# A fifth quad by seven products in the gate/up pairs, its low parts made by GpSimd, the residual parked in DRAM

## The reference

```python
for l in range(DEPTH):                                  # DEPTH = 2
    h = rmsnorm(x, norm_mix[l])
    q, k, v, gate_b, gate_c, u = split(h @ w_in[l])     # 2048 x 6144
    o_attn = diff_attention(rope(q), rope(k), v, lam)   # 8 heads, then a sub-norm
    o_conv = short_gated_conv(gate_b, gate_c, u, conv_w[l])
    x = x + concat(o_attn, o_conv) @ w_out[l]           # 2048 x 2048
    h = rmsnorm(x, norm_ffn[l])
    x = x + (silu(h @ w_gate[l]) * (h @ w_up[l])) @ w_down[l]   # 2048 x 5632, twice; 5632 x 2048
return rmsnorm(x, norm_final)
```

## Time and profile before

| | |
|---|---|
| runs | 2156.14, 2156.8, 2157.34 us |
| profiled execution, span from first to last instruction | 2155.3 us |
| TensorE, VectorE, ScalarE, GpSimd busy | 2144.2, 1771.7, 1218.7, 314.5 us |
| weights and all else read from memory | 448.65 MB, 209 GB/s |
| granted TensorE clock, mean | 0.999 |

### The profile page before, as it was taken

The page is one execution under the profiler, slowest core; times in us unless marked ns, Lnnn a source line. Parts: engine busy times, 40 slices in busy tenths (PEclk is TensorE's granted clock), DMA queues, the critical chain, the costliest instruction groups (busy, mean ns, idle before and its releaser), DMA issues.

```text
span 2155.3 us, 27924 instructions
## 1 busy us (share of the span) xinstructions
PE 2144.2 (99%) x10397; PEld 1794.4 (83%) x10397; DVE 1771.7 (82%) x2143; ACT 1218.7 (57%) x1714; POOL 314.5 (15%) x310
## 2 busy tenths in 40 slices
PE   9999999999999999999999999999999999999998
PEld 7888888888888888888888888888888888888886
DVE  5776676899899988999866666768998998988997
ACT  6454455666566555556554555546665665655564
POOL 0031120211221110000001211201112112100010
PEclk9999999999999999999999999999999999999999
DMA  9654445777777776767766444557777777756685
GB/s 349 203 183 176 176 157 189 212 218 223 246 217 229 227 229 205 227 216 221 246 200 217 171 161 157 176 194 212 218 229 232 219 222 244 221 198 219 219 240 181
DMA packets 152872, 456.81 MB, mean 212 GB/s; under 512 B 17440, under 2 KB 18080, under 8 KB 152352
## 3 DMA queue, kind: packets, MB, share of 16 engines
q1 hardware_dynamic: 132624, 416.41, 55.5%
q0 software_dynamic: 18816, 35.66, 9.8%
q10 hardware_dynamic: 1296, 2.94, 0.4%
HBM read 448.65 MB, written 2.10 MB: 209 GB/s over the span
## 4 chain that ended last, share of the span: by engine, by line
PE 97%; DVE 1%; ACT 1%; DMA 1%; POOL 0%; issue 0%; ACTq 0%; SPq 0%; DVEq 0%
PE bank L1861 16%; PE bank L1863 16%; PE bank L1862 16%; PE bank L1835 14%; PE bank L1875 9%; PE bank L1874 9%; PE bank L1873 9%; PE bank L1838 7%; PE bank L2039 1%; PE bank L1998 1%; PE bank L2021 1%; PE bank L1977 0%; DMA raw<-w_gu_dram 0%; POOL o_rms L675 0%; DVE wlo L1191 0%; PE bank L2007 0%
## 5 line engine op out<-in xcount | busy, mean ns | idle before, releaser
L761 ACT ACTIVATE whi<-raw 128x1024 fp32r<-128x1024 f32 x540 | 553.9, 1056 | 195.2 <-PE bank L1863 137.4
L1184 DVE TENSOR_TENSOR wlo<-raw,whi 128x1024 fp32r<-128x1024 f32 x504 | 606.9, 1229 | 65.9 <-ACT whi L761 64.9
L767 ACT ACTIVATE whi<-raw 128x1024 fp32r<-128x1024 f32 x480 | 430.0, 944 | 241.7 <-DVE raw L1206 139.6
L1191 DVE TENSOR_TENSOR wlo<-raw,whi 128x1024 fp32r<-128x1024 f32 x480 | 501.0, 1084 | 49.7 <-ACT whi L767 46.4
L1835 PE MATMUL bank<-xg,whi 128*128 128x512 f32 x1280 | 406.9, 399 | 1.0 <-DVE wlo L1440 1.0
L1861 PE MATMUL bank<-whi,xg 128*128 128x512 f32 x864 | 339.3, 393 | 0.5 <-DVE wlo L1184 0.5
L1863 PE MATMUL bank<-whi,xg 128*128 128x512 f32 x864 | 336.7, 390 | 0.0
L1862 PE MATMUL bank<-wlo,xg 128*128 128x512 f32 x864 | 336.5, 389 | 0.0
L1838 PEld LDWEIGHTS bank<-xg,wlo 128*128 128x128 f32 x1280 | 240.5, 188 | 56.9
L1838 PE MATMUL bank<-xg,wlo 128*128 128x256 f32 x1280 | 252.0, 278 | 0.0
L1835 PEld LDWEIGHTS bank<-xg,whi 128*128 128x128 f32 x1280 | 195.0, 189 | 3.3 <-DVE xg L1434 1.4
(11 more groups left out here) (161 smaller groups left out, 3050.7 us busy)
## 6 DMA issues: line engine op xcount, KB each, us to landing
raw<-w_gu_dram SPq DMA_DIRECT2D x268, 512.0 KB, 4.9
raw<-w_in_dram SPq DMA_DIRECT2D x188, 512.0 KB, 4.5
raw<-w_down_dram SPq DMA_DIRECT2D x140, 512.0 KB, 5.4
raw<-w_gu_dram SPq DMA_DIRECT2D x168, 256.0 KB, 4.2
raw<-w_out_dram SPq DMA_DIRECT2D x64, 512.0 KB, 4.4
raw<-w_gu_dram POOLq DMA_DIRECT2D x84, 256.0 KB, 5.7
raw<-w_down_dram SPq DMA_DIRECT2D x72, 256.0 KB, 4.7
raw<-w_down_dram POOLq DMA_DIRECT2D x36, 256.0 KB, 6.1
```

Of the source, the lines that this page charges most:

```text
L761: act.activation(whi[:, blk.slot(k)], raw[:, slot, half * UNIT_KT:(half + 1) * UNIT_KT, :], ACT.Copy).then_inc(hi_ready, 1)
L767: act.activation(whi[:, quad.slot(n), 0:tiles.stop - tiles.start], raw[:, quad.raw(), tiles, :], ACT.Copy).then_inc(hi_ready, 1)
L1184: dve.tensor_tensor(wlo[:, blk.slot(k)], raw[:, slot, half * UNIT_KT:(half + 1) * UNIT_KT, :], lo_bits(whi[:, blk.slot(k)]), ALU.subtract) ...
L1191: dve.tensor_tensor(wlo[:, quad.slot(n), into], raw[:, quad.raw(), tiles, :], lo_bits(whi[:, quad.slot(n), into]), ALU.subtract).then_inc( ...
```

## The change

`GU_SEVENS` becomes 5. Pairs 1 to 8 (`GU_FIVES`) get a list of their own, `gu_five`: units 5 to 7 of both blocks plain and five quads. Pair 0 and pair 9 keep four quads, pair 10 two.

- **GpSimd** makes ten low parts in each of pairs 1 to 8: all six plain units, and the last of the second parts of quads 0 to 3 (`split_last`). In pair 0 it makes four, right 5, left 6, left 7 and right 7. The wait for the copy of the sum stays in pair 9 alone.
- **Joint first parts**: in pairs 0 to 9 the three tiles of the first products are split by one instruction on ScalarE and one on VectorE (`quad.joint`).
- **Ring of tiles**: `whi` and `wlo` are ten tiles, given out by written lists (`GU_FIVE_TILES` and others), since a split now has two or three tiles.
- **Two more places for loads** (`raw_gu`) lie over the residual. For that, ScalarE's queue writes the residual (2 MB) to DRAM in pair 0; SP waits for it ahead of the loads of pair 1, and reads it back ahead of the loads of pair 10; the first `fold` of the down stage waits for it.
- **The forms of the fifth quad** are a third batch with one quad, made within pair 0.

```diff
-GU_SEVENS = 4
+GU_SEVENS = 5
+GU_FIVE_ORDER = [("left", 5), ("right", 5), ("first", 0), ("first", 1), ("left", 6), ("second", 0), ("first", 2),
+                 ("right", 6), ("second", 1), ("first", 3), ("second", 2), ("first", 4), ("second", 3), ("second", 4),
+                 ("left", 7), ("right", 7)]
+GU_FIVES = range(1, NGU // 2 - 2)
...
+    raw_gu = at("raw_gu", [P, NRAW_GU - NRAW, LOAD_KT, COLS], F32, resid_at)
+    resid_kept = nc.dram_tensor("resid_kept", (DEPTH, P, QT, DM), F32, kind="Internal").ap()
...
+                if isinstance(blk, Pair) and blk.name == "gu" and blk.i == GU_FIVES[0]:
+                    sp.wait_ge(resid_out, 16 * (blk.layer + 1))
...
+                    sp.dma_start(resid[:], resid_kept[blk.layer]).then_inc(resid_back, 16)
...
+            def split_last(quad):
+                tiles = plan.span[quad.split[-1]]
+                pool.wait_ge(hi_ready, quad.split[-1] + 1)
+                pool.tensor_tensor(wlo[:, tiles], raw_place(quad.raw())[:, 0:2, :], lo_bits(whi[:, tiles]), ALU.subtract
+                                   ).then_inc(pool_weights_ready, 1)
...
-                for p in GU_FOURS:
-                    prior, pair = (plan.pairs[layer, "gu", n] for n in (p - 1, p))
-                    add_b(pair.quads[0])
-                    split_first_units(prior, pair)
-                    for k in range(1, len(pair.quads)):
-                        add_b(pair.quads[k])
+                for p in GU_FIVES:
+                    pair, later = (plan.pairs[layer, "gu", n] for n in (p, p + 1))
+                    left, right = pair.blocks
+                    split(left, 5)
+                    split(right, 5)
+                    add_b(pair.quads[2])
+                    split(left, 6)
+                    split_last(pair.quads[0])
+                    add_b(pair.quads[3])
+                    split(right, 6)
+                    split_last(pair.quads[1])
+                    add_b(pair.quads[4])
+                    split_last(pair.quads[2])
+                    split_last(pair.quads[3])
+                    add_b(later.quads[0])
+                    split(left, 7)
+                    if later.five:
+                        add_b(later.quads[1])
+                    split(right, 7)
...
+            def gu_five(pair, prior):          # VectorE
+                q = [pair.quads[k] for k in range(GU_SEVENS)]
+                layer, before = prior.layer, [b.i for b in prior.blocks]
+                gates_ups(prior, 0, 1)
+                gates_ups(prior, 1, 0)
+                gates_ups(prior, 1, 1)
+                hidden_products(layer, before[0], 0)
+                hidden_products(layer, before[0], 1)
+                first_parts(q[0])
+                hidden_products(layer, before[1], 0)
+                hidden_products(layer, before[1], 1)
+                hidden_low(layer, before[0])
+                first_parts(q[1])
+                sums_of(q[0])
+                hidden_low(layer, before[1])
+                second_part(q[0])
+                sums_of(q[1])
+                first_parts(q[2])
+                second_part(q[1])
+                sums_of(q[2])
+                first_parts(q[3])
+                second_part(q[2])
+                sums_of(q[3])
+                first_parts(q[4])
+                sums_of(q[4])
+                second_part(q[3])
+                second_parts(q[4])
+                gu_fold(pair)
+                gates_ups(pair, 0, 0)
```

## The result

The changed kernel takes 2373.22 us (median of 4 runs, 2372.32 to 2373.98) against 2157.07 for the kernel before on the same chip: a ratio of 1.1004, 95% interval 1.0988 to 1.1019. The direction was right, the size was not: 2261 was forecast, with a range up to 2350. The profiled execution has a span of 2370.5 us.

What follows compares the result with a forecast made beforehand. TensorE bounds the kernel; with five quads, VectorE and GpSimd taking turns on SBUF make 16 pairs 48.0 us instead of 41.75. 2155.3 + 100 + 4 for parking = 2259, plus 1.5 to the runs' median: 2261 us, range 2178 to 2350.

Steps and rivals of the forecast that it cites:

- VectorE 3.5 us behind: Gate/up pair of the kernel before: TensorE fills 41.75 us, VectorE is busy 38.25 of them.
- The saving: Pairs with five quads: fewer matmuls save 10.9 us in all; with nothing in the way a pair takes 41.07 us.
- Turns: VectorE's two-SBUF-input work and GpSimd's subtractions go one after the other, 2.24 us each; six hold VectorE up by 13.4 us.
- Then TensorE has half of a second product set and both last units, 30 matmuls, 6.8 us: End of a five-quad pair: TensorE's work after VectorE's last second part, added to VectorE's stretch for 47.5 us a pair.
- VectorE's 27.3 + 13.4: From last gate/up addition to last second part: 27.3 us of VectorE work, plus 13.4 held by six GpSimd subtractions.
- Nothing, at most 3: First pair of each layer: 35 us of added work in a 42.3 us window costs nothing, at most 3 us a layer.
- Parking: Residual's way to DRAM and back, 2 MB each way per layer: 1 us for each of four transfers, +4 us, ends 0 and 40.
- (a): Rival, six subtractions in VectorE's stretch: GpSimd fits VectorE's pauses, the saving stands, 2146 us, at most 2150; chance 0.13.
- (b): Rival, same six subtractions: each costs VectorE 1.1 to 2.0 us; at 1.5, 43.5 us a pair, 2188 us; chance 0.10.
- (c): Rival: VectorE keeps GpSimd out, TensorE waits for GpSimd, late DMA additions hold sums; 55 us a pair, 2373; chance 0.09.
- What would show it: Signs in five-quad pairs: GpSimd subtractions over 3 us on average, VectorE's over 1.3, some near 3.5, sum copies 48 us apart.
- 302.26: Trace time in the kernel before: a two-element GpSimd operation was done only at 305.93, past two VectorE subtractions begun after it.

Runs made afterwards that it cites:

- x_before_none: The kernel before, with GpSimd's two low parts of unit 4 in pairs 1 to 9 given to VectorE: 2176.57 us, ratio 1.0092.
- x_none: The changed kernel with all low parts of pairs 1 to 8 on VectorE, GpSimd only starting its additions by DMA: 2216.7 us, ratio 1.0277.
- x_before_late: The kernel before, with GpSimd making the two low parts of unit 6, beside VectorE's sums, instead of those of unit 4: 2222.32 us, ratio 1.0304.
- x_fill2: The changed kernel with 28 meaningless matmuls in TensorE's two long waits of each of pairs 1 to 8: 2333.4 us, ratio 1.0819.
- x_writes: The changed kernel with GpSimd's subtractions in pairs 0 to 8 replaced by two writes of zero that read nothing: 2149.95 us, ratio 0.997.

## Why the prediction was wrong in size

**The bound.** "VectorE 3.5 us behind" was too much: 1.2 us were to be had (x_before_none). It entered no sum, but the kernel before is VectorE's nearly as much as TensorE's, and a quad does not relieve VectorE: by the prediction's own times it costs 1.68 + 0.60 + 1.14 + 2.28 = 5.7 us where the two plain units that it replaces need two low parts, 2.3. The runs without GpSimd agree: 43.57 us of VectorE a pair with five quads (x_none), 40.2 with four (x_before_none).

**The saving** is right: 41.23 us a pair where nothing is held, against 41.07.

**Turns** are right in price. Six subtractions hold VectorE up by 13.0 us, forecast 13.4; in x_before_late one costs 2.24, the forecast's own figure. In these rows whoever comes second waits out the rest of the other's instruction. By the exclusive lock that the Trainium skill states (SBUF — State Buffer, Who interferes with whom) the prediction had estimated 49.4 us a pair; the pairs measure 52.1 at full clock and 54.6 as they are, so neither sum of one resource is the time.

**The step that failed** is "Then TensorE has half of a second product set and both last units, 30 matmuls, 6.8 us", added to VectorE's 27.3 + 13.4 without a wait, at full clock: 47.5. Go round the cycle from one last gate/up addition of a pair to the next, by way of the low part that TensorE waits for at 639.57, the second part of quad 3. The rows of VectorE, in the kernel after and in x_fill2, where the clock is full:
```profile
597.81 0.69 DVE L1415 TENSOR_TENSOR gate_up<-bank,gate_up 128x512 f32<-128x512 f32 x1 [0.22 <-PE bank L2029]
...
638.30 1.21 DVE L1308 TENSOR_TENSOR wlo<-raw,whi 128x1024 fp32r<-128x1024 f32 x1
...
652.44 0.69 DVE L1415 TENSOR_TENSOR gate_up<-bank,gate_up 128x512 f32<-128x512 f32 x1 [0.22 <-PE bank L2029]
```
```profile
485.79 0.69 DVE L1415 TENSOR_TENSOR gate_up<-bank,gate_up 128x512 f32<-128x512 f32 x1 [0.22 <-PE bank L2029]
486.40 1.47 DVE L1722 SCALAR_TENSOR_TENSOR ev<-gate_up,rms_tok,ev 128x256 f32<-128x256 f32 x2
...
498.03 1.23 DVE L1308 TENSOR_TENSOR wlo<-raw,whi 128x1024 fp32r<-128x1024 f32 x1 [0.58 <-ACT whi L852]
...
525.40 1.21 DVE L1308 TENSOR_TENSOR wlo<-raw_gu,whi 128x1024 fp32r<-128x1024 f32 x1
...
537.88 0.69 DVE L1415 TENSOR_TENSOR gate_up<-bank,gate_up 128x512 f32<-128x512 f32 x1 [0.22 <-PE bank L2029]
```

| us | by the forecast's terms | x_fill2 | kernel after |
|---|---|---|---|
| last addition to the end of quad 3's last part | 27.3 + 13.4 - 2.4 = 38.3 | 40.8 | 41.7 |
| from there to the next last addition | 48 x 0.227 = 10.9 | 11.3 | 12.9 |
| pair | 49.2 | 52.1 | 54.6 |

So three terms lie in the 7.1 us between 47.5 and 54.6:

- The backlog, +1.7 us. Held, VectorE delivers its last three low parts in a burst from 638.30 on. What decides is the first of them: behind it TensorE has 48 matmuls, not 30, and the two parts after it (2.4 us of VectorE) hide. That makes 49.2 in place of 47.5.
- Waits and holds that the sum left out, +2.9 us (49.2 to 52.1). In x_fill2 two gated products are held as well (1.47 us in place of 0.87, by one of the four subtractions placed beside the fold; in the kernel after a wait of 0.63 us for ScalarE stands there instead), VectorE waits 0.58 us for a high part that ScalarE makes behind a held sum, and each of the five `other_sums` starts some 0.79 us after its `first_sum` (the hold not counted), where 0.60 had been taken: 2.2 us together. The other 0.7 are small. These parts were read in the trace and not taken out singly.
- The clock, +2.5 us, shown by x_fill2 (52.1 to 54.6). 1.6 of them are TensorE's slowed matmuls behind 639.57. Most of the other 0.9 is the wait at 627.49: TensorE, slowed, frees a tile late, ScalarE fills it late, and VectorE waits (read in the trace).

In the spans the miss is 215.2 - 104 = 111 us: 16 x 6.6 over the 48.0 taken are 106, the parking taken at 4 for nothing takes 4 off, and about 9.6 lie in pairs 0 and 1. Pair 0 ends 3.9 us later in the first layer and 2.5 in the second, where "Nothing, at most 3" was forecast, and pair 1 takes 57.1 and 56.0.

**Parking**: 4 us taken, 0 measured.

**The rivals.** (a) and (b) fall: a held sum ends only after the 1024-column subtraction has ended, and waits 2.0 to 2.4 us for it. (c) has the measured time, 2373, but not its way: VectorE does not keep GpSimd out (2.7 us a subtraction), the additions by DMA hold nothing, and TensorE waits for VectorE. That the time agrees is chance.

**What would show it**: VectorE's sums at up to 3.65 us came; GpSimd's "over 3 us on average" did not (2749 and 2655 ns), which already tells that it is not an even taking of turns.

## What to carry to other kernels

GpSimd looked idle at 15%, but it was free only where its reads of SBUF did not meet VectorE's two-input reads. Place its subtractions by what VectorE does at that moment, and price each one that meets a VectorE instruction at nearly its whole length (2.24 of 2.39 us here). A sum of busy times gives no time for a pair in which three engines hand on to each other; go round the cycle, with every wait in it, and ask at which delivery the last consumer still has most to do. An engine's unused time is slack only after the waits of its own cycle are taken off.

## What the runs showed of the hardware

- It is mostly VectorE that waits: GpSimd's subtractions stretch by 0.3 us (2406 to some 2700 ns), VectorE's held instructions by 2.0 to 2.4 us. GpSimd started first in all six cases of the pair shown, since its tile was ready while VectorE was still in the instruction before; 302.26 is the other case. GpSimd waits, too: five of these six came into a VectorE instruction and ended 2.22 to 2.28 us after the end of that instruction.
- GpSimd's writes of the same tiles cost VectorE nothing that shows (x_writes: sums of 685 ns beside memsets of 0.96 to 0.99 us).
- After waits of 2.8 and 4.4 us the granted clock fell within 1 us of the restart and stayed down for some 3 us; together 2.5 us a pair (against x_fill2). Behind a wait of 1.40 us in x_fill2 it was still 1.00.
